# One encoder layer on one core: attention by head pairs, token-major mLSTM with a ones column, three modulation batches and an earlier bias split

## What is computed

```python
mod = jax.nn.silu(c) @ w_ada + b_ada          # c: one row per sequence; 6 x 1024 columns
sh1, sc1, ga1, sh2, sc2, ga2 = split(mod, 6)
h = rmsnorm(x, g_norm1) * (1.0 + sc1) + sh1
u = h @ w_in                                  # 1024 x 3592
q, k = rmsnorm per head of sb_q, sb_k         # 8 heads of 64; v = sb_v
z = q.k / 8 ; mask = key position < query position
a = exp(log_sigmoid(z) + sum over later keys of log_sigmoid(-z)), o_sb = a @ v
mq, mk = silu(causal_conv(ml_qk, width 4))    # 4 heads of 128; mv = ml_v
# mLSTM, exact and chunkwise: S = (mq.mk) * w_intra ; num = S @ mv + w_inter * C q
# den = sum S + w_inter * n.q ; h = num / max(|den|, exp(-m)) ; C, n, m are outputs
o_ml = sigmoid(ml_o) * rmsnorm(h_ml, g_head)
x = x + ga1 * (concat(o_sb, o_ml) @ w_out)
h2 = rmsnorm(x, g_norm2) * (1.0 + sc2) + sh2
x = x + ga2 * moe(h2)                         # top-4 of 32 experts, each 1024 -> 2048 -> 1024
```

## Time and profile before

| | |
|---|---|
| median of 3 runs | 1361.68 us (1358.65 to 1362.62) |
| the profiled execution's own time | 1363.36 us |
| its span, first to last instruction | 1361.2 us |
| mean granted TensorE clock | 0.925 of full speed |
| busy: PE, PEld, DVE, ACT, POOL | 1164.1, 548.0, 379.6, 212.5, 49.3 us |
| moved by DMA | 455.34 MB, mean 335 GB/s |

### The profile page before, as it was taken

The page is one execution under the profiler, slowest core; times in us unless marked ns, Lnnn a source line. Parts: engine busy times, 40 slices in busy tenths (PEclk is TensorE's granted clock), DMA queues, the critical chain, the costliest instruction groups (busy, mean ns, idle before and its releaser), DMA issues.

```text
span 1361.2 us, 21887 instructions
## 1 busy us (share of the span) xinstructions
PE 1164.1 (86%) x7341; PEld 548.0 (40%) x7342; DVE 379.6 (28%) x1055; ACT 212.5 (16%) x450; POOL 49.3 (4%) x56
## 2 busy tenths in 40 slices
PE   3899998895387797879999999899999989869995
PEld 2677776663132232224433344344333333313431
DVE  1103534522313222321142222222232222322133
ACT  1423242212201100001111101101111111001010
POOL 0001110003500000000000000000000000000000
PEclk8899998787598988989999999989999999999998
DMA  9934216526089999999999998998999999999991
GB/s 358 387 105 148 63 62 228 222 78 221 1 349 416 419 418 418 419 416 417 401 412 418 419 418 343 419 417 351 417 417 417 418 419 418 418 418 417 417 406 59
DMA packets 102598, 455.34 MB, mean 335 GB/s; under 512 B 10044, under 2 KB 14780, under 8 KB 69692
## 3 DMA queue, kind: packets, MB, share of 16 engines
q1 hardware_dynamic: 94608, 448.03, 82.0%
q10 hardware_dynamic: 7948, 6.73, 1.7%
HBM read 451.56 MB, written 3.17 MB: 334 GB/s over the span
## 4 chain that ended last, share of the span: by engine, by line
PE 68%; DMA 14%; SPq 6%; DVE 5%; issue 4%; POOL 2%; ACT 1%; DVEq 0%; ACTq 0%
PE psum L830 25%; PE psum L856 13%; PE psum L552 9%; DMA ring<-w_gu 7%; SPq L478 5%; PE psum L875 4%; DMA ring<-w_down 3%; PE psum L740 3%; PE psum L799 2%; DMA ring<-w_ada 2%; PE psum L807 1%; PE psum L521 1%; DVE work L1485 1%; DVE work L1489 1%; PE psum L823 1%
## 5 line engine op out<-in xcount | busy, mean ns | idle before, releaser
L830 PE MATMUL psum<-ring,work 128*32 128x512 f32 (+2 forms) x2048 | 430.9, 622 | 26.5 <-DMA ring<-w_gu 25.8
L830 PEld LDWEIGHTS psum<-ring,work 128*32 128x32 f32 (+2 forms) x2048 | 132.9, 134 | 276.0 <-issue 206.2
L856 PE MATMUL psum<-ring,work 128*32 128x256 f32 (+2 forms) x1504 | 217.9, 480 | 10.5 <-DMA ring<-w_down 10.4
L1500 DVE TENSOR_TENSOR work<-psum,work 128x320 f32<-128x320 f32 x256 | 109.9, 484 | 230.0 <-PE psum L875 229.0
L932 ACT ACTIVATE work<-psum 128x256 f32<-128x256 f32 (+5 forms) x206 | 88.1, 444 | 353.2 <-PE psum L856 224.8
L856 PEld LDWEIGHTS psum<-ring,work 128*32 128x32 f32 (+2 forms) x1504 | 88.0, 130 | 124.8 <-issue 91.7
L1470 DVE TENSOR_SCALAR work<-csb 96x128 bf16<-96x128 f32 x64 | 15.4, 280 | 416.6 <-PE psum L830 415.7
L552 PE MATMUL psum<-h,ring 128*128 128x320 f32 x448 | 126.5, 440 | 1.2 <-ACT h L976 1.2
L1147 ACT ACTIVATE work<-work 128x128 f32<-128x128 f32 (+2 forms) x64 | 25.2, 393 | 568.6 <-DVE work L1484 567.3
L552 PEld LDWEIGHTS psum<-h,ring 128*128 128x128 f32 x448 | 85.7, 193 | 37.0 <-issue 1.6
L875 PE MATMUL psum<-work 32*128 32x320 f32 (+2 forms) x512 | 82.7, 486 | 1.1 <-ACT work L932 1.0
(11 more groups left out here) (233 smaller groups left out, 701.0 us busy)
## 6 DMA issues: line engine op xcount, KB each, us to landing
ring<-w_gu SPq DMA_DIRECT2D x256, 1024.0 KB, 18.5
ring<-w_down SPq DMA_DIRECT2D x128, 1024.0 KB, 20.1
ring<-w_ada SPq DMA_DIRECT2D x12, 2048.0 KB, 9.7
ring<-w_in SPq DMA_DIRECT2D x7, 2048.0 KB, 21.3
ring<-w_out SPq DMA_DIRECT2D x2, 2048.0 KB, 8.4
x<-xT ACTq DMA_DIRECT2D x1, 1280.0 KB, 13.4
yT<-h SPq DMA_DIRECT2D x4, 320.0 KB, 2.2
work<-b_exp ACTq DMA_DIRECT2D x3, 384.0 KB, 12.0
```

Source lines behind the costliest of these rows:

```text
L830: last = mm(o, xg[:, kk, 0:m], cols(ring[:, kk, :]), start=False, stop=kk == KD - 1)
L856: last = mm(o, actT[:, kk, 0:m], ring[:, GU_UNITS + kk // 2, c1_:c1_ + n], start=False, stop=kk == 7)
L1500: tt_(t_, bank[SPREAD_BANKS[u]][:, 0:T], t_, ALU.add).then_inc(acc_ready, 1)
```

## The change

- **Modulation.** w_ada is read in 12 chunks of 2 blocks of rows by 2048 columns (8 KB in one piece), and 4 chunks accumulate one batch of 16 feature blocks: 3 batches instead of 4. The stationary operand is 32 columns wide, 30 of them zeros; the moving one 512. One copy empties a batch. Batches 2 and 3 both run around the mLSTM; none is left behind w_out.
- **Values per token.** v and mv are projected with h as the stationary operand, so they come out token-major: 3 units each in place of 4 (128, 128 and 64 tokens; the last one in two halves of 64 partitions). The turning of v and mv goes away.
- **Head pairs.** Attention runs over 4 pairs. Scores of the two heads alternate between the upper and lower 64 partitions, a @ v between the two halves of 64 output partitions; ScalarE, VectorE and GpSimd take 128 x 1024 at once; the columns are reordered so that a mask is one instruction of 2 x 320.
- **Token-major mLSTM.** mv carries a column of ones, C the column n: numerator and denominator come out of the same matmuls as 128 tokens x 129, and C with n too. The reciprocal is 128 x 3; the sum of squares is a VectorE reduction; the hidden state is turned back by TensorE (`ml_turn`). Weights and scores have two buffers.
- **Biases.** b3 gets its own place. b_exp is loaded behind the first h, and the split stands first in POOL's stream.
- The loads of the key and value cache move behind the first h; c0 and c0T become one load of 128 x 4 x 129.

The core of the diff:

```diff
-            for c in range(4):
-                ada(2, c)
+            for j in range(ADA):
+                ada(j, 2)
...
-                for kk in range(KD):
+                for u in range(2):
+                    kk = 2 * j + u
                     for g in range(4):
-                        last = mm(bank[bk][32 * g:32 * g + 2, c * P:(c + 1) * P], cs[:, kk, :], w[:, kk, g * P:(g + 1) * P],
-                                  start=kk == 0, stop=kk == KD - 1)
+                        last = mm(bank[bk][32 * g:32 * g + 32, :], cs[:, kk, :], w[:, u, g * CHC:(g + 1) * CHC], start=kk == 0, stop=kk == KD - 1)
...
+            def z_of(p):
...
+                for k0, q0, nq, cols in ((0, 0, 256, AC), (128, 128, 128, B), (256, 256, 64, E)):
+                    for u in range(2):
+                        r = slice(64 * u, 64 * u + 64)
+                        mm(bank[2 + u][:, cols], k[r, p, k0:k0 + 128], q[r, p, q0:q0 + nq], start=True, stop=True)
...
+            z_of(0)
...
+            proj()
+            proj()
+            between_of(0)
+            proj()
+            proj()
+            av_of(0)
+            z_of(1)
...
+            z_of(2)
+            proj_tokens(0)
+            between_of(2)
+            proj_tokens(1)
+            proj_tokens(2)
+            av_of(2)
+            z_of(3)
+            proj()
+            proj()
+            between_of(3)
+            proj()
+            proj()
+            pe.wait_ge(zmin_ready, 4)
+            turn_k()
+            pe.wait_ge(proj_done, 17)
+            ada(0, 0)
+            av_of(3)
...
+                mm(o[:, 0, :], S_[:, A], mvx[:, 0, i, 0:VN], start=True, stop=True)
+                mm(o[:, 1, :], S_[:, C], mvx[:, 0, i, 0:VN], start=True, stop=False)
+                mm(o[:, 1, :], S_[:, B], mvx[:, 1, i, 0:VN], start=False, stop=True)
+                mm(o[0:64, 2, :], S_[0:64, E], mvx[0:64, 2, i, 0:VN], start=True, stop=False)
+                mm(o[0:64, 2, :], qw, C0n[:, i, 0:VN], start=False, stop=True).then_inc(num_ps, 1)
...
+            for part in range(3):
+                act_.dma_start(b_stage[part * NE:(part + 1) * NE, :], b_exp).then_inc(ld_bias, 16)
...
-            act_.wait_ge(state_stored, 16 * 3)
-            for part in range(3):
-                act_.dma_start(b_stage[part * NE:(part + 1) * NE, :], b_exp).then_inc(ld_bias, 16)
...
-            mod_rows(3, 4)
...
-            mod_of(3, 7, mod3_ready)
```

More of the change, by code:

```diff
@@ L94, in __call__, with build @@
         self.wait()
-def build(nc, xT, small, const, b_exp, kcT, vc, c0, c0T, w_ada, w_in, w_out, w_gu, w_down,
-          yT, koT, voT, convo, co, no, mo):
+def build(nc, xT, small, const, b_exp, kcT, vc, c0n, w_ada, w_in, w_out, w_gu, w_down,
+          yT, koT, vo, convo, cno, mo):
     ctx = ExitStack()
@@ L503, in _, with chunk @@
             used = [0]
-            def chunk():
+            def chunk(halves=False):
                 n = used[0]
@@ L582, in _, with turn_k @@
+            def turn_k():
+                pe.wait_ge(mkq_ready, 1)
+                for tt, (t0, n) in enumerate(TILES):
+                    for c in range(4):
+                        last = nc.tensor.transpose(bank[(2, 3, 7)[tt]][0:n, c * P:(c + 1) * P], mk[:, c, t0:t0 + n], ident)
+                    last.then_inc(ktr_ps, 1)
+            z_of(0)
             pe.wait_ge(gtok_ready, 1)
@@ L733, in _ @@
+            ml_scores(0)
+            ada(1, 0)
+            ml_scores(1)
+            ada(2, 0)
+            ml_values(0)
+            ada(3, 0)
+            ml_scores(2)
+            ml_values(1)
+            ada_turn(1, 7)
+            ada(0, 0)
+            ml_turn(0)
+            ml_scores(3)
+            ada(1, 0)
+            ml_values(2)
+            ml_turn(1)
+            ada(2, 0)
+            ml_values(3)
+            ml_turn(2)
+            ada(3, 0)
+            ml_turn(3)
             for t in range(8):
@@ L744, in _ @@
             pe.wait_ge(x1_ready, 16)
-            for c in range(2):
-                ada(4, c)
             assert used[0] == PRE
@@ L1000, in nrs @@
                 rstd(scr[:, 2 + i % 2, 0:T], bank[6 + i % 2][:, 0:T], SBD, nrs_ready)
-            act_.wait_ge(v_init, 4)
-            for t in range(12):
+            act_.wait_ge(v_init, 3)
+            for t in range(11):
                 proj_out(t)
@@ L1043, in _ @@
-            act_.wait_ge(proj_done, 20)
+            proj_out(11)
+            proj_out(12)
+            weights_exp(0)
+            proj_out(13)
+            proj_out(14)
+            z_terms(1)
+            proj_out(15)
+            proj_out(16)
+            weights_exp(1)
+            proj_out(17)
+            proj_out(18)
+            act_.wait_ge(proj_done, 11)
+            with nc.allow_non_contiguous_dma(reason="three columns of each row"):
+                act_.dma_start(cv[:, :, 0, :], raw[:, :, TP:TP + 3]).then_inc(conv_stored, 16)
+                act_.dma_start(cv[:, :, 1, :], raw[:, :, RAWW - 3:RAWW]).then_inc(conv_stored, 16)
@@ new lines, in _ @@
+            z_terms(2)
+            proj_out(19)
+            weights_exp(2)
+            proj_out(20)
+            proj_out(21)
+            act_.wait_ge(conv_ready, 8)
+            act_.wait_ge(conv_stored, 32)
+            fn(sgy, y, ACT.Sigmoid).then_inc(sgy_ready, 1)
+            ln_exp_tables()
+            z_terms(3)
+            proj_out(22)
+            proj_out(23)
+            weights_exp(3)
+            proj_out(24)
+            proj_out(25)
+            act_.wait_ge(proj_done, 18)
```

709 lines of the change are left out of this document (355 added, 354 removed).

## The result

The changed kernel takes **1317.82 us** (median of 4 runs, 1317.04 to 1318.67) against 1362.15 of the kernel before beside it: a ratio of 0.9667, 95% interval 0.9648 to 0.9685. The forecast was 1302.5 us. The direction and the range held, the range near its upper end; the gain is 44 us where 59 were forecast. The time alone lies nearer to two of the rivals (1309.5 without the overlap of halves, 1314 with another wait in the router) than to the forecast; it is the stages that tell them apart. Most of this part is about the missing 15.

The account below looks back on a forecast made before the run. Bound by a 366.4 us chain, then a DMA-busy expert stage of 994.8 us carried over unchanged. Terms -5 - 11.2 - 1 - 19.4 + 1.1 - 23.7 = -59.2 took the median 1361.68 to 1302.5 us; range 1291 to 1320.

Parts of the forecast that it names:

- without the overlap of halves: Rival in attention: products in different halves of the array do not overlap, attention 7.0 us longer, 1309.5 us; chance 0.10.
- another wait in the router: Rival in the router: POOL's clearing of acc or ACT's copies keeps half of the 23.7 us, 1314 us; chance 0.07.
- Start, -5 forecast: Start to first projection: faster w_ada, later caches and one copy for four save 5 us; bounds -3 and -7.
- "-1.9" for the rate: Start: w_ada in 8 KB pieces moves 8.39 MB in 20.2 instead of 22.1 us.
- second limit: Start: the first w_in chunk arrives 5.5 us after w_ada and limits the first projection at about 35.5 us.
- To the first broadcast, -1 forecast: Attention's end to first mLSTM broadcast: one earlier load, DVE's copies leave 3 us of 4.0; bounds -2 and +3.
- Attention, -11.2 forecast: Attention: 95 us against 106.2, with halves overlapping and 1.3 us added for PE gaps; bounds -12.5 and -4.2.
- mLSTM, -19.4 forecast: mLSTM: 43 us against 62.4, from 33 of PE work, 5 of waits, 5 for lower clock; bounds -24 and +5.
- Out-projection, +1.1 forecast: Out-projection: the turn of the third modulation batch behind its first tile adds 1.1 us.
- Router, -23.7 forecast: Router: bias split moved earlier, so DVE goes on at 329.1 instead of 352.87 us; bounds -23.7 and -20.
- Rival 5: Attention: the bias split on POOL delays the first mask if b_exp lands after 89 us, making the kernel slower; chance 0.02.
- a low clock throughout the mLSTM: Rival in the mLSTM: all of it at 1.2 GHz, 43 us becomes 68, 1327 us in all; chance 0.10.

Follow-up runs that it names:

- the four together: Changed kernel with x first on SP's queue, c0n issued early, gate products in three rows, modulation rows of batch 2 copied early: 1294.3 us, ratio 0.9482.

## Why the prediction was right, and where it failed

- **Start, -5 forecast, +0.9 measured.** The step that failed is "-1.9" for the rate: it was priced by w_ada alone, and the loads beside it were left where they had been. The rate did come (417 GB/s from 5 to 30 us, where the earlier trace rows had 379). But a larger piece also takes a larger share of the engines, and x, whose sum of squares stands ahead of the fourth chunk in PE's order, went from 13.4 to 26.3 us. With x first the forecast's 35.5 is met (35.45), so the rest of the term stands; its second limit, the first w_in chunk, is the wait ahead of 35.38 with the four together.
- **To the first broadcast, -1 forecast, +5.4 measured.** The step was "one load of the same size issued some 6 us ahead of the end of attention". It was issued 3.8 us ahead (198.98; the last values end at 202.8), as ACT reaches it behind its last projection copy, and half a us behind a w_ada chunk, with the next one 2.7 us behind it; it took 13.0 us where the loads before took 6.5 and 7.8. The same size was not the same load: its pieces had gone from 2 KB to 516 bytes, four times as many, and those beside it from 2 to 8 KB. The upper bound of +3 was too narrow for the same reason as at the start. The 9 idle us also cost the mLSTM some 3 to 4, seen when they went.
- **Attention, -11.2 forecast, -8.2 measured.** Overlap of the halves, the part left open, is shown. The wait ahead of the fourth pair is 0.93, inside the 1.3 allowed. The 3 us missing (1.8 when the changed kernel was run again) are not in a step of the sum but in its assumption that PE stays at a clock of 1.00, which the earlier trace rows showed for the stage before only from 108.5 on: the changed kernel runs from about 103 to 113 us at the lower level (104 to 111 when run again), the kernel before for some 3 us. Both have the row of gate products ahead of it. That it is this row is shown (with it split, the clock stays); why the lower level lasts longer after the change, and not always as long, is not.
- **mLSTM, -19.4 forecast, -19.9 measured.** The stage is 42.5 for 43, with one wait for the modulation rows of 2.89 (forecast 4) and about 5 us lost to the lower level, at its begin and behind that wait, as allowed. The sum had 33, 5 and 5 us for TensorE's work, its waits and the clock; measured are some 33.5, 3.5 and 5.5, so the stage came out by its terms and not by luck. How much of it is the ones column, the smaller reciprocal or the shorter state products was not tried apart.
- **Out-projection, +1.1 forecast, -1.6 measured.** The turn costs 0.60 at the full clock; the 1.1 was read from a row behind a wait, at the lower one. What was left out: the stage before ran at 0.94 of the full clock behind a wait of 2.58, now at 1.00. That this is all of it was not tried.
- **Router, -23.7 forecast, -23.4 measured**, and shown from the other side by putting 18 us back.
- **Experts, 0 forecast, +0.6 measured**, inside their scatter.
- **The biases** land by 58.5 us, well ahead of 89; the split runs from 58.5 to 79.6 beside the projections. Rival 5 had no ground.

The rivals on halves, on a low clock throughout the mLSTM and on the router did not come; what came, loads crowded out by larger pieces, was none of them.

## What to carry to other kernels

A transfer whose pieces are made larger also takes a larger share of the engines from what runs beside it: list which small loads are in flight beside it, on another queue, and when each is needed, before the gain is booked. Put what is needed first on the same queue ahead of the bulk, or issue it before the bulk; that cost nothing here and gave back some 8 and 10 us. And price a PE wait with the lower clock behind it: 2.9 us of waiting cost 5 to 6.

## What the runs showed that was not expected

- Smaller pieces made the kernel 11 us faster (1306.92 against 1317.8) while the bandwidth fell (360 against 382 GB/s over the first 36 us): what the small loads beside them gained was worth more than the rate.
- Two queues that both have work pass about the same number of packets, whatever the size: 281 and 281, 737 and 738, 303 and 321, and 448 and 526 with 2 KB beside 516 bytes.
- 5.6 us of products with 8 moving columns, with PE busy throughout, were followed by 7 to 10 us at a granted clock of 0.50 in the changed kernel; the same 24 products in three rows were not.
